# Two first weight packs in halves between the x tiles, and a small DVE chain moved behind the low parts of x

## What is computed

```python
def rms_norm(x, g):
    xf = x.astype(jnp.float32)
    y = xf * lax.rsqrt(jnp.mean(xf * xf, axis=-1, keepdims=True) + EPS)
    return (y * g.astype(jnp.float32)).astype(x.dtype)

def swiglu(h, w_in, w_out):
    gu = h @ w_in
    gate, up = gu[..., :D_FF], gu[..., D_FF:]
    return (jax.nn.silu(gate) * up) @ w_out

x = x + 0.5 * swiglu(rms_norm(x, g[0]), ffn_w_in[l, 0], ffn_w_out[l, 0])
```

## Time and profile before

| | |
|---|---|
| median of 3 runs | 1871.6 us (1871.47 to 1871.76) |
| profiled execution, its own time | 1870.33 us |
| its span, first to last instruction | 1868.5 us |
| PE busy | 1820.4 us, 97% |
| PE weight load busy | 1497.1 us, 80% |
| DVE busy | 954.2 us, 51% |
| ACT busy | 634.9 us, 34% |
| POOL busy | 310.6 us, 17% |
| mean granted TensorE clock | 0.973 of full speed |

### The profile page before, as it was taken

One profiled execution on the slowest core, in us unless ns is written; L12 is line 12 of the kernel. 1 busy time (PEld: TensorE's weight loads), 2 busy tenths in 40 slices (PEclk: granted clock), 3 DMA queues, 4 the chain that ended last, 5 costly groups with the idle time before them and its releaser, 6 DMA issues.

```text
span 1868.5 us, 21481 instructions
## 1 busy us (share of the span) xinstructions
PE 1820.4 (97%) x8136; PEld 1497.1 (80%) x8136; DVE 954.2 (51%) x1117; ACT 634.9 (34%) x856; POOL 310.6 (17%) x270
## 2 busy tenths in 40 slices
PE   8999999979999999999999999999989999999997
PEld 6878888858988888888888888888766788888886
DVE  7678968535445543443355443434496354434333
ACT  6332232334333333332234333322425343323222
POOL 7884633014202200000100000000100100000000
PEclk9999999986599999999999999999999999999999
DMA  5345544666332322222222222223310222222321
GB/s 197 108 149 161 166 145 146 229 221 220 85 112 81 111 90 101 93 98 100 92 91 102 100 91 101 91 101 98 111 57 1 91 90 96 95 101 90 102 90 46
DMA packets 80834, 207.77 MB, mean 111 GB/s; under 512 B 24032, under 2 KB 34400, under 8 KB 79744
## 3 DMA queue, kind: packets, MB, share of 16 engines
q1 hardware_dynamic: 68656, 188.81, 30.2%
q0 software_dynamic: 2784, 14.29, 2.3%
q10 hardware_dynamic: 9328, 3.77, 0.8%
HBM read 183.77 MB, written 23.07 MB: 111 GB/s over the span
## 4 chain that ended last, share of the span: by engine, by line
PE 87%; DVE 5%; POOL 2%; issue 2%; ACT 2%; DMA 2%; SPq 0%; ACTq 0%; DVEq 0%; POOLq 0%
PE bank L1562 26%; PE bank L1564 26%; PE bank L1563 26%; PE bank L1751 1%; PE bank L1744 1%; DMA s_u<-x_gained 1%; PE bank L1734 1%; PE bank L1862 1%; PE bank L1864 1%; PE bank L1881 1%; DVE w_split L1124 1%; ACT w_split L726 1%; PE bank L1632 1%; DMA w_raw<-wstream 0%; PE bank L1873 0%
## 5 line engine op out<-in xcount | busy, mean ns | idle before, releaser
L1124 DVE TENSOR_TENSOR w_split<-w_raw,w_split 128x1024 fp32r<-128x1024 f32 x299 | 392.5, 1317 | 638.1 <-ACT w_split L726 637.3
L1562 PE MATMUL bank<-h_split,w_split 128*128 128x512 f32 x1512 | 591.8, 391 | 5.6 <-DVE w_split L1124 3.1
L1564 PE MATMUL bank<-h_split,w_split 128*128 128x512 f32 x1512 | 588.5, 389 | 0.0
L1563 PE MATMUL bank<-h_split,w_split 128*128 128x512 f32 x1512 | 588.3, 389 | 0.0
L726 ACT ACTIVATE w_split<-w_raw 128x1024 fp32r<-128x1024 f32 x299 | 315.3, 1058 | 676.2 <-PE bank L1564 650.4
L1562 PEld LDWEIGHTS bank<-h_split,w_split 128*128 128x128 f32 x1512 | 284.0, 188 | 67.4 <-issue 3.1
L1562 PE MATMUL bank<-g_split,w_split 128*128 128x512 f32 (+1 forms) x854 | 329.7, 386 | 2.9 <-DVE w_split L1124 2.3
L1563 PEld LDWEIGHTS bank<-h_split,w_split 128*128 128x128 f32 x1512 | 284.0, 188 | 59.6 <-issue 1.2
L1564 PEld LDWEIGHTS bank<-h_split,w_split 128*128 128x128 f32 x1512 | 283.8, 188 | 59.2
L1563 PE MATMUL bank<-g_split,w_split 128*128 128x512 f32 (+1 forms) x854 | 328.4, 385 | 0.0
L1564 PE MATMUL bank<-g_split,w_split 128*128 128x512 f32 (+1 forms) x854 | 328.3, 384 | 0.0
(11 more groups left out here) (284 smaller groups left out, 1275.6 us busy)
## 6 DMA issues: line engine op xcount, KB each, us to landing
w_raw<-wstream SPq DMA_DIRECT2D x299, 512.0 KB, 3.5
op_slot<-s_ops SPq DMA_DIRECT2D x5, 2048.0 KB, 9.3
s_ops<-ops_out SPq DMA_DIRECT2D x16, 512.0 KB, 3.2
op_slot<-s_ops POOLq DMA_DIRECT2D x3, 2048.0 KB, 14.0
s_ops<-c_pow POOLq DMA_DIRECT2D x8, 512.0 KB, 5.1
s_ops<-k_window SPq DMA_DIRECT2D x64, 64.0 KB, 3.4
x_res<-xT SPq DMA_DIRECT2D x8, 256.0 KB, 7.5
s_u<-x_gained ACTq DMA_DIRECT2D x8, 256.0 KB, 3.2
```

The lines of the kernel that those rows point to most:

```text
L1124: tt(W[:, r, 1, :], RAW[:, r, :], W[:, r, 0, :].bitcast(F32), ALU.subtract).then_inc(s_lo, 1)
L1562: mm(bank, hi, x_hi, start=start, stop=True, skip_group_check=True)
L1563: mm(bank, hi, x_lo, start=False, stop=True, skip_group_check=True)
L1564: return mm(bank, lo, x_hi, start=False, stop=True, skip_group_check=True)
```

## The change

The first two packs are no longer loaded whole. SP issues the first halves of both (columns 0 to 511, the weight tiles of x0 to x3) behind x0, and the second halves of both behind x3. ACT and DVE split them in the same order, halves behind k = 0 and behind k = 3. PE waits for the first halves at k = 0 and for the second halves at k = 4. On DVE the small chain with its memset now stands behind the low parts of x and the splits of packs 0 to 3, ahead of the additions of squares. `s_lo` counts packs 0 and 1 when their second halves are done.

```diff
@@ block.sync
             for k in range(DT):
                 sp.dma_start(X[:, k, :], xT[k]).then_inc(s_xin[k], 16)
-                if k < 2:
-                    sp.dma_start(RAW[:, k, :], wstream[k]).then_inc(s_raw[k], 16)
+                if k == 0:
+                    for r in range(2):
+                        sp.dma_start(RAW[:, r, 0:512], wstream[r][:, 0:512]).then_inc(s_half_in[r], 16)
+                if k == 3:
+                    for r in range(2):
+                        sp.dma_start(RAW[:, r, 512:], wstream[r][:, 512:]).then_inc(s_raw[r], 16)
@@ block.scalar
                 h_hi(k, G_IN0A, H)
-                if k < 2:
-                    split(FFN0A1, k - AHEAD)
+                if k == 0:
+                    for r in range(2):
+                        act.wait_ge(s_half_in[r], 16)
+                        nc.scalar.activation(W[:, r, 0, 0:512], RAW[:, r, 0:512], ACT.Copy).then_inc(s_half_hi, 1)
+                if k == 3:
+                    for r in range(2):
+                        act.wait_ge(s_raw[r], 16)
+                        nc.scalar.activation(W[:, r, 0, 512:], RAW[:, r, 512:], ACT.Copy).then_inc(s_hi, 1)
@@ block.vector
             dve.wait_ge(s_args, 1)
+            for k in range(DT):
+                h_lo(k, G_IN0A, H, H_BASE[FFN0A1])
+                if k == 0:
+                    for r in range(2):
+                        dve.wait_ge(s_half_hi, r + 1)
+                        tt(W[:, r, 1, 0:512], RAW[:, r, 0:512], W[:, r, 0, 0:512].bitcast(F32),
+                           ALU.subtract).then_inc(s_half_lo, 1)
+                if k == 3:
+                    for r in range(2):
+                        dve.wait_ge(s_hi, r + 1)
+                        tt(W[:, r, 1, 512:], RAW[:, r, 512:], W[:, r, 0, 512:].bitcast(F32), ALU.subtract).then_inc(s_lo, 1)
+            split(FFN0A1, 2 - AHEAD)
+            split(FFN0A1, 0)
             ts(S6[:, 13, :], LAM[:, 1, :], col(C_SGN), None, ALU.mult)
...
             nc.vector.memset(KT[:, :, 0:T - 1, :], 0.0).then_inc(s_zero_taps, 1)
-            for k in range(DT):
-                h_lo(k, G_IN0A, H, H_BASE[FFN0A1])
-                if k < 2:
-                    split(FFN0A1, k - AHEAD)
-            split(FFN0A1, 2 - AHEAD)
-            split(FFN0A1, 0)
             for k in range(1, DT):
                 dve.wait_ge(s_sq0, k + 1)
@@ block.tensor, first_pair
                     for q in range(2):
-                        if k == 0:
+                        if k == 0 and stage == FFN0A1:
+                            pe.wait_ge(s_half_lo, q + 1)
+                        elif k == (4 if stage == FFN0A1 else 0):
                             pack(stage + q)
```

More of the change, by code:

```diff
@@ L218, in build @@
     s_xin = [sem(f"x_loaded{i}") for i in range(DT)]
+    s_half_in = [sem(f"first_half_loaded{i}") for i in range(2)]
+    s_half_hi, s_half_lo = sem("first_half_hi"), sem("first_half_lo")
     s_bc, s_cpst, s_pos = [sem("bc_even_loaded"), sem("bc_odd_loaded")], sem("c_op_stored"), sem("positions_loaded")
```

## The result

The changed kernel took 1874.84 us (median of 13 runs, 1872.70 to 1876.34), the kernel before, run beside it, 1871.47 (median of 13, 1869.86 to 1873.05): ratio 1.0018, 95% interval 1.0010 to 1.0027. It is 3.4 us slower (1.9 to 5.1). The forecast was +3.8 in a range from 1870.5 to 1878.0. The profiled execution after took 1873.47 us, span 1871.6: 3.1 more than the profiled one before.

What follows compares the result with a forecast made beforehand. PE, busy 97%, was taken to bound the kernel, its start set by DVE's sums. 0 + 0 + 2.2 + 1.6 = +3.8 us on 1870.3 gave 1874.1, with 1.3 to the median 1875.4; range 1870.5 to 1878.0.

Steps and rivals of the forecast that it cites:

- What bounds the start: At the first stat PE's first pair (ready 22.06) meets DVE's sums behind pack 3 (ready 24.0); the sums decide.
- Rival E: At the start: the earlier first pair is worth its 3 us, 1868.6; wants the stat no later than 21; chance 0.05.
- The halves on the DMA queue: Loads at the start: same bytes ahead of pack 3, so it lands at 16.25 again, 0 us.
- the bound of 1: Pack 3's landing: SP's two more issues could delay it by about 1 us if issue, not bandwidth, set it.
- a sign of being wrong: Pack 3's landing: the forecast is wrong if it lands at another time by more than 0.5.
- The small chain: On DVE, now between pack 3's low part and the first addition, on the path that decides: +2.2 us.
- The clock: PE idle 7.4 us before the first stat instead of 2.0, so the granted clock falls: +1.6 us, bounds 0 to 2.7.
- Nothing paid back: The wait of 2.84 us before block 2's turn gives nothing back; b_bar of block 1 is late by the same 3.8.
- Rival A: At block 2's turn: 0.8 to 4.0 us paid back, so -0.2 to +3.0, in the middle 1873.0; chance 0.25.
- A's smaller figure: At block 2's turn: 0.8 us back, the lower end of what is paid back, making +3.0.
- A's larger figure: At block 2's turn: 4.0 us back, the clock not falling below a wait of some 2.1, making -0.2.
- The first pair: PE's first matmuls at the start run without a break and end at about 18.9, 3 us earlier, worth nothing.

Runs made afterwards that it cites:

- e1: The changed kernel with the small chain left where it was, ahead of x on DVE; packs 0 and 1 in halves: ratio 1.0013 to the kernel before.
- e4: The changed kernel with the small chain behind the seven additions of squares, ahead of the low parts of packs 4 and 5: ratio 1.0011 to the kernel before.
- e6: The changed kernel with squares and six additions ahead of packs 2 and 3's splits, PE adding the eighth square, small chain behind them: ratio 1.0002 to the kernel before.
- a2_after_again: The changed kernel, unchanged, measured again in a later set of 5 rounds: ratio 1.0022 to the kernel before.
- e3_warm: The changed kernel with 7 matmuls of ones on PE between the first pair and the wait for the sums: ratio 1.0014 to the kernel before.
- e2_chain_only: The kernel before, packs 0 and 1 whole, with only the small chain moved behind the splits of packs 0 to 3: ratio 1.0012.
- e5: e4 with 4 matmuls of ones on PE between the first pair and the wait for the sums: ratio 1.0014 to the kernel before.
- e10: The changed kernel with block 1's b_bar at tile 4 of FFN0A1 instead of tile 5: ratio 1.0003 to the kernel before.
- e8: The kernel before with one table entry changed, block 1's b_bar at tile 4 of FFN0A1 instead of tile 5: ratio 0.9991.
- e9: e6 with block 1's b_bar at tile 4 of FFN0A1 instead of tile 5: ratio 0.9993 to the kernel before.
- e7: Same order of squares, additions, small chain and mean as e6, but packs 0 and 1 whole as in the kernel before: ratio 1.0004 to it.
- b2: The kernel before, unchanged, run again as a kernel under test: ratio 1.0001.

## Why the prediction was right

*What bounds the start.* The two paths that meet at the first stat were the right ones, and the stat moved as the second: 26.60 against 26.3 forecast. e1 and e4 take the chain out of its place and the stat is back at 24.5 and 24.2. PE's first pair being off the path, its 2.3 us are worth nothing, as written. Rival E, which would have it worth its time once the stat comes by 21, asked for too little: in e6 the stat comes at 20.6 and the time is that of the kernel before.

*The halves on the DMA queue.* The step that put this at 0 was too low. It was argued from bandwidth: the same bytes ahead of pack 3. In four profiles with whole packs pack 3's high part starts at 15.87 to 16.25, mean 16.02; in seven with halves and the same order of ACT at 16.33 to 17.16, mean 16.71. So the halves cost 0.7 us, inside the bound of 1 that the prediction drew from SP's issues: pack 3 is issued at 8.3 instead of 7.3. Whether the two more DMAs or their new places in the queue make it, no run tells. Between the two profiles that were compared it was 0.35; in a2_after_again it was 0.9, more than the 0.5 that the prediction had set as a sign of being wrong. The Trainium skill (DMA: Bandwidth & Descriptors, Anatomy of one DMA) gives a fixed part of about 2 us for each DMA, on the path of DMAs issued by GpSimd; these are SP's. By that figure an estimate for two of them one after the other is 4 us; the runs show a third of a us for each.

*The small chain.* +2.2 forecast; 2.22 by its own rows, 2.15 at the stat (2.50 less the landing's 0.35).

*The clock.* +1.6 forecast, 2.1 measured (4.61 less 2.50), and e3_warm, which keeps the clock up, gives 2.0; in a2_after_again it was 1.7. The mechanism was right; the size was taken from a shorter low stretch at the turn of block 2. (The rows put that stretch from 132.9 to 136.3, not to 136.15; no term uses it.)

*Nothing paid back.* This step was wrong. The forecast let the lag pass to the end, with the wait before the turn of block 2 unchanged. Rival A named the sign against it, b_bar of block 1 more than 0.8 us earlier against PE, and it came: POOL gets b_bar 3.46 late where PE is 4.61 late, 1.15 earlier, and all of that is the DVE split that meets POOL's operations, 1.14 us shorter. The wait shrank by 0.8, as A's smaller figure said, and the time came out just above A's upper end of +3.0. A's larger figure was out: the clock fell there behind a wait of 2.02, though A wanted it to hold below 2.1. Nor would holding have paid: in e2_chain_only it held behind 2.01, and PE then waited 1.69 us for the low part of g instead of 0.57. The lag shrank by another 0.1 to the turn of block 3 and 0.6 to the S5 stat; the last is no more than what two profiles of the kernel before differ by on the same stretch.

*The sum.* The terms were 0.8 too small at the start (4.6 of lag for 3.8), and 1.0 of the 4.6 was given back by block 3, 1.5 by the end, where the forecast had nothing given back. That the total of 3.4 came within half a us of the 3.8 is partly luck: the errors had opposite signs.

*The first pair* ended at 19.8 (its last matmul started at 19.56), not 18.9: the second first-half landed at 7.35 and x1 at 8.5, 1.0 and 0.8 later than the 6.34 and 7.73 that I took.

*That a lag passes on in full* holds for small lags and not for large ones. From the turn of block 0 to that of block 3, lags of 1.6, 2.0 and 2.65 (e4, e1, e3) became 1.6, 1.8 and 2.5; lags of 3.45, 4.6 and 4.8 (e2 and the changed kernel twice) became 2.6, 3.6 and 4.0. Only e5 grew, from 1.6 to 2.1. The ratios of e1 to e5, 2.1 to 2.6 us, are too coarse to show it.

## What to carry to other kernels

Before moving work to let an engine start earlier, find where its path meets the next one, and which of the two is late there: work moved onto the late side costs all of its time there, the early side gains nothing, and an engine that waits longer may come back at a lower clock. Look next at where the schedule last waits for another engine, for a start that is gained in full is still lost there (e6), and a large lag is partly absorbed there (e10). One table entry at such a wait (e8) gave a lower time than the whole rearranged start (e6), though by less than the intervals tell apart.

## What the runs showed of the hardware

The granted clock fell behind waits of very different length. In the kernel before it stayed at 1.00 through a wait of 1.9 us at 22 to 24, in e2_chain_only it fell to 0.50 after one of 2.08 at the same place. The turn of block 2 shows it more plainly: the clock fell with a wait of 2.02 before the turn (the changed kernel) and stayed with 2.01 (e2) and 2.50 (e9); it fell with each of the eight waits from 2.67 to 3.41, and stayed with 1.14 (e8). So between 2.0 and 2.5 us the length of the wait alone does not tell. In the first pair with whole packs, where PE stands idle twice for 1.1 to 2.4 us around three matmuls, it fell in four profiles of five (e2, e7, e8, b2) and delayed the pair's end by 1.4 to 1.7 us; with halves it fell in none of nine. So the same program can run this stretch at either of the two levels.

How long a DVE operation with two SBUF inputs takes hangs on what POOL does beside it: the split that took 3.69 us from 83.75 took 2.55 from 88.36 in the changed kernel and 4.28 from 85.34 in e5, against 1.23 undisturbed. In all three it ends 1.1 us behind the end of a POOL operation, which fits a wait for POOL and then its own time: 87.44 behind 86.36, 90.91 behind 89.83, 89.62 behind 88.53. The POOL operations, in the kernel before, the changed kernel and e5, with e5's split:

```profile
84.10 2.26 POOL L553 TENSOR_TENSOR c_pow<-bc_in_odd,lam_pow_signed 128x1152 f32<-128x1152 f32 x1
```
```profile
86.27 3.56 POOL L561 TENSOR_TENSOR c_pow<-c_pow,s_tmp 128x1152 f32<-128x1152 f32 x1
```
```profile
86.27 2.26 POOL L559 TENSOR_TENSOR c_pow<-bc_in_odd,lam_pow_signed 128x1152 f32<-128x1152 f32 x1
```
```profile
85.34 4.28 DVE L1136 TENSOR_TENSOR w_split<-w_raw,w_split 128x1024 fp32r<-128x1024 f32 x1 [3.92 <-ACT w_split L732]
```

That fits what the Trainium skill says (SBUF — State Buffer, SBUF: two separate sides), that one of the two blocks the other for a whole instruction. POOL's products stand at the same time in the kernel before and in the changed one (81.87 and 81.71) while DVE is 4.6 us later, so DVE meets fewer of them. It is why 0.8 us of the lag is gone at the turn of block 2.
